# Experts stage: the low parts of the down weights computed by VectorE instead of GpSimd, and VectorE's step in another order

## The reference

```python
h = modulate(rmsnorm(x, norm_ffn), sh2, sc2)
s = sigmoid(h @ w_router)                      # 64 scores; 4 of 8 groups, then 6 experts for each token
gates = sel / sum(sel) * 2.5
routed[token] += gate * (silu(h @ w1[e]) * (h @ w3[e])) @ w2[e]      # for each of the 6 experts
shared = (silu(h @ ws1) * (h @ ws3)) @ ws2
x = x + g2 * (routed + shared);  out = rmsnorm(x, norm_final)
```

## Time and profile before

| | |
|---|---|
| three runs, us | 2855.18 (median), 2844.31, 2860.29 |
| profiled execution, us | 2856.53 |
| its span, us | 2854.9 |
| mean granted clock of TensorE | 0.955 of 2.4 GHz |
| busy, us (share of span) | TensorE 2541.4 (89%), VectorE 1692.9 (59%), GpSimd 1364.5 (48%), ScalarE 1014.7 (36%) |
| HBM | 224 GB/s over the span |

### The profile page before, as it was taken

How to read it: one execution, slowest core, us unless ns; L and a number is a source line. 1 busy time by engine, 2 the same in 40 slices (tenths; PEclk the granted TensorE clock), 3 DMA queues, 4 the chain that set the end, 5 groups by cost and what they waited for, 6 DMA issues and landing times. The chain is left out here.

```text
span 2854.9 us, 52119 instructions
## 1 busy us (share of the span) xinstructions
PE 2541.4 (89%) x11953; PEld 2029.2 (71%) x11954; DVE 1692.9 (59%) x2579; ACT 1014.7 (36%) x1615; POOL 1364.5 (48%) x1136
## 2 busy tenths in 40 slices
PE   7999999999849899589999999999998999989991
PEld 4787777777638777478777777777776788767780
DVE  4664554574236777554855575675588644686643
ACT  3212433323212222212543353443356422453422
POOL 1210025612245666421655665665577644576644
PEclk9999999999969999699999999999999999999995
DMA  7775768574456554445986887987799866698747
GB/s 274 305 259 203 265 214 309 196 276 166 163 209 232 170 202 159 149 111 139 340 258 162 248 274 191 271 268 190 200 282 351 285 168 155 183 317 259 209 105 270
DMA packets 247800, 641.42 MB, mean 225 GB/s; under 512 B 32876, under 2 KB 46512, under 8 KB 232240
## 3 DMA queue, kind: packets, MB, share of 16 engines
q1 hardware_dynamic: 188736, 459.72, 44.8%
q0 software_dynamic: 58992, 180.78, 25.9%
HBM read 463.08 MB, written 177.33 MB: 224 GB/s over the span
## 5 line engine op out<-in xcount | busy, mean ns | idle before, releaser
L2154 DVE TENSOR_TENSOR w_exp_lo<-w_exp,w_exp_hi (+1 forms) x256 | 401.8, 1604 | 74.5 <-ACT w_exp_hi L2093 65.5
L2093 ACT ACTIVATE w_exp_hi<-w_exp (+1 forms) x256 | 260.9, 1056 | 220.4 <-issue 130.5
L2280 PE MATMUL ps_h<-w_exp_hi,x_exp_t_hi 128*128 (+1 forms) x1216 | 312.6, 399 | 26.1 <-ACT w_exp_hi L2093 20.3
L2010 POOL TENSOR_TENSOR w_exp_lo<-w_exp,w_exp_hi (+1 forms) x130 | 321.9, 2500 | 13.2 <-ACT w_exp_hi L2097 10.1
L2280 PE MATMUL ps_h<-w_exp_lo,x_exp_t_hi 128*128 (+1 forms) x1216 | 311.6, 398 | 16.9 <-DVE w_exp_lo L2154 16.9
L2280 PE MATMUL ps_h<-w_exp_hi,x_exp_t_lo 128*128 (+1 forms) x1216 | 321.6, 407 | 0.0
L2280 PEld LDWEIGHTS ps_h<-w_exp_hi,x_exp_t_hi 128*128 128x128 f32 x1216 | 228.1, 189 | 88.9 <-ACT w_exp_hi L2093 20.5
L2070 POOL DMA_INDIRECT sum_d<-w_shared_raw,give x136 | 246.1, 1810 | 91.1 <-DVE w_shared_raw L2192 42.9
L2280 PEld LDWEIGHTS ps_h<-w_exp_lo,x_exp_t_hi 128*128 128x128 f32 x1216 | 228.4, 189 | 77.2 <-issue 22.6
L1134 PE MATMUL ps_p<-wa_hi,hx_split 128*128 128x512 f32 x1088 | 279.1, 403 | 4.1 <-DVE kvqg_out L100 3.2
L2060 POOL DMA_DIRECT2D give<-list_d x136 | 76.7, 564 | 399.2 <-issue 391.6
(11 more groups left out here) (270 smaller groups left out, 4390.6 us busy)
## 6 DMA issues: line engine op xcount, KB each, us to landing
w_exp<-in_experts SPq DMA_DIRECT2D x386, 512.0 KB, 7.6
hx_split<-hx_d SPq DMA_DIRECT2D x54, 1024.0 KB, 5.7
rec_m<-rec_d SPq DMA_DIRECT2D x16, 1536.0 KB, 8.8
hx_d<-hx_split SPq DMA_DIRECT2D x18, 1024.0 KB, 5.5
wm_rest<-in_w_mod_rest POOLq DMA_DIRECT2D x16, 1024.0 KB, 5.9
rec_d<-kvqg_out SPq DMA_DIRECT2D x48, 256.0 KB, 4.4
xt<-in_xt POOLq DMA_DIRECT2D x18, 512.0 KB, 8.8
rec_d<-kt_kvf_out SPq DMA_DIRECT2D x32, 256.0 KB, 5.4
```

The source lines that it names most:

```text
L2010: pool.tensor_tensor(w[1][:, piece(e, i)].bitcast(F32R), raw(e, i), w[0][:, piece(e, i)], ALU.subtract).then_inc(wd_lo, 1)
L2093: act.activation(w[0][:, piece(e, i)].bitcast(F32R), raw(e, i), ACT.Copy).then_inc(gu_hi, 1)
L2154: dve.tensor_tensor(w[1][:, piece(e, i)].bitcast(F32R), raw(e, i), w[0][:, piece(e, i)], ALU.subtract).then_inc(gu_lo, 1)
L2280: last = pe.matmul(out, x[:, j * P:(j + 1) * P].bitcast(F32R), w_part[:, bass.ds(w_at + j * stride, 512)].bitcast(F32R), start=(start and ...
```

## The change

The splits of the down weights (`split`) leave GpSimd's program and come to VectorE's as `split_d`. VectorE's order in step k becomes: pieces 0 and 1; weighing of tile k - 2; low part of h of tile k - 1; piece 2; gating; low part of x; piece 3; then, where tile k - 1 was the first of its expert, the two down pieces. VectorE therefore looks up the change at k - 1 too. The last two tiles are weighed behind the loop.

```diff
@@ gpsimd
-            def split(e, i):
-                pool.wait_ge(wd_hi, e * N_D + i - N_GU + 1)
-                pool.tensor_tensor(w[1][:, piece(e, i)].bitcast(F32R), raw(e, i), w[0][:, piece(e, i)],
-                                   ALU.subtract).then_inc(wd_lo, 1)
-
-            for i in range(N_GU, N_GU + N_D):
-                split(0, i)
...
-            for i in range(N_GU, N_GU + N_D):
-                split(1, i)
...
             def step(k, par, r):
-                before = change(pool, k - 1) if not isinstance(k, int) or k > NT else None
                 gather(k + 2, par, r + 1)
                 load_take(k + 3, 1 - par, r + 1 + par)
-                if before is not None:
-                    at_change(pool, before, split, range(N_GU, N_GU + N_D))
@@ vector
+            def split_d(e, i):
+                dve.wait_ge(wd_hi, e * N_D + i - N_GU + 1)
+                dve.tensor_tensor(w[1][:, piece(e, i)].bitcast(F32R), raw(e, i), w[0][:, piece(e, i)],
+                                  ALU.subtract).then_inc(wd_lo, 1)
...
                 here = change(dve, k)
-                at_change(dve, here, split, range(3))
+                before = change(dve, k - 1) if not isinstance(k, int) or k > 0 else None
+                at_change(dve, here, split, range(2))
+                if not isinstance(k, int) or k > 1:
+                    weigh(k - 2, par, None if isinstance(k, int) else r - 1)
                 if not isinstance(k, int) or k > 0:
                     copy_ht(k - 1, 1 - par)
+                at_change(dve, here, split, range(2, 3))
...
                 at_change(dve, here, split, range(3, N_GU))
                 if not isinstance(k, int) or k > 0:
-                    weigh(k - 1, 1 - par, None if r is None or (isinstance(k, int) and k == NT) else r - (1 - par))
+                    wait(dve, d_done, k - 1)
+                    at_change(dve, before, split_d, range(N_GU, N_GU + N_D))
...
             for i in range(N_GU):
                 split(0, i)
+            for i in range(N_GU, N_GU + N_D):
+                split_d(0, i)
             n = iterations(dve, step, after)
+            weigh(n * 2 + (NT - 2), 0, n - 1)
             copy_ht(n * 2 + (NT - 1), 1)
             weigh(n * 2 + (NT - 1), 1, n - 1)
```

## The result

The changed kernel took 2907.14 us (median of 4 runs, 2900.46 to 2911.72) against 2857.73 us for the kernel before on the same chip (4 runs). The ratio is 1.0181, 95% interval 1.0142 to 1.0219: slower. I had forecast 2836 us and a range up to 2880; the time that came lies 5 us from the one that rival B gave, 2912.

What follows compares the result with a forecast made beforehand. TensorE, busy 89%, was taken to lose 145 us at expert changes in the routed part. Waits of -11 us times 1.6 gave -18; with -3.4 (start) and +2 (loads) some -19, so 2836 us, range 2804 to 2880.

Steps and rivals of the forecast that it cites:

- rival B: Step after each change step outside long runs: gather behind the late weighing, 68 us of waits, 2912 us; chance 0.22.
- The lock of VectorE and GpSimd: VectorE's weight subtractions: GpSimd's subtractions stop them; 97 us of waiting in VectorE's busy time go, maximum below 1.3 us.
- VectorE's added work and the start: VectorE takes 130 more subtractions, busier by about 62 us net; the wait at 1222.70, ahead of the routed part, shrinks: -3.4 us.
- Low part of the weights: TensorE's 16.9 us of waits for VectorE's low part of the weights: -8 us, ends 0 and -16.9.
- Saturated runs: Long runs of expert changes: VectorE ends the down subtractions later than GpSimd did, +9 us of waits, ends -5 and +36.
- Register loads: VectorE's lookup of the step before, two loads more a step: mostly hidden, 2 us, bounds 0 and 69.
- Low part of h: TensorE's waits for VectorE's low part of h: -12 us in all, ends 0 and -39.2.
- Gather: TensorE's 33.8 us gather wait: -20 from GpSimd's freed time, +20 (ends 0 and +80) from the weighing behind two subtractions.
- The price of a wait, 1.6: Routed part: one us of TensorE wait costs 145/90 = 1.6 us of time.

Runs made afterwards that it cites:

- e2: The kernel before with only VectorE's new order; the down subtractions stay on GpSimd, two lookups a step: 1.0301 of the kernel before.
- e7: The changed kernel with the weighing of tile k - 2 ahead of pieces 0 and 1, still behind the four lookups: 0.9954 of the kernel before.
- e13: The changed kernel with the weighing first in VectorE's step, ahead of the lookups and of pieces 0 and 1: 0.9864 of the kernel before.
- e4: The kernel before with two more lookups a step on VectorE, result unused, nothing else: 1.0048 of the kernel before.
- e3: The changed kernel with 3 + 1 lookups in a round of two steps instead of 4 + 4: 1.0048 of the kernel before.
- e1: The kernel before with the down subtractions moved to VectorE, its old order kept (weighing last, behind them), four lookups a step: 0.9953 of the kernel before.
- e11: e16's kernel with a memset of 2.4 us on GpSimd ahead of each gather: 0.9875 of the kernel before.
- e14: e16's kernel with a memset (1.83 us median) on GpSimd ahead of each scatter, behind its wait for the weighing: 1.0257 of the kernel before.
- e15: As e14 with the memset ahead of each scatter half as long, 0.98 us: 1.0027 of the kernel before.
- e16: e1 with 3 + 1 lookups in a round instead of 4 + 4, no memset: 0.9886 of the kernel before.
- e8: The changed kernel with GpSimd issuing the gather one tile further ahead, before the scatter instead of behind it: 1.0663 of the kernel before.

## Why the prediction was wrong

*The lock of VectorE and GpSimd: right.* All 256 gate and up subtractions now take 1211 to 1228 ns; in e2, where GpSimd keeps its own, the longest takes 6077. The rule of the Trainium skill ("SBUF — State Buffer", Who interferes with whom) that the prediction used agrees with both.

*VectorE's added work and the start: right in the main.* GpSimd's busy time is down by 318 us (320 forecast). VectorE's is up by 37 (62 forecast); its weight subtractions alone take 58 more by the view's lines (306.9 + 153.1 for 401.8), and the rest I did not trace. The wait of TensorE at its first down products fell from 7.78 to 2.87 us, but its wait for ScalarE's high part of x before that grew from 2.01 to 4.53; together the shared expert's steps are 2.5 us shorter, for my 3.4.

*Low part of the weights: better.* I took -8 of the 16.9 us; all of it went.

*Saturated runs: smaller.* I took +9 us of waits, some 14 us of time; the run of 11 is 130.3 us for 130.6, and all eight long runs together are 2.8 us longer.

*Register loads: failed, the second cause.* I counted two added loads per step and took 2 us, since the pieces that followed the lookups had no idle time ahead. I did not ask what the reorder makes of the loads that were there. The first piece starts at a median of +3.0 to +4.3 in the change steps of the kernel before, the changed one, e7 and e13, whatever stands ahead; the weighing can start at +0.2, and the change put it behind the loads in every step, quiet ones too. In the rows of the changed kernel that is 4.58 us without work; moved ahead of them (e7 to e13) the weighing gives 0.9% back, some 25 us. The loads that were added cost their own share besides (e4: 0.5%, 14 us, inside my bounds of 0 and 69).

*Low part of h: failed.* I took -12; it came out +3. e3 and e7 show what held it up: with fewer lookups it is 11.2 us, with the weighing ahead of the pieces 23.7. The gain was there, and the lookups and the weighing ahead of it ate it; I had charged 0.2 to 0.3 us for the second and nothing for the first.

*Gather: the step that failed.* The term was -20 for GpSimd's freed time and +20 for the late weighing, together 0; it measured +53.8. Of the first part e1 shows 6 us in the old order (33.8 to 27.7), and the changed kernel against e2 13 to 18 in the new one. The second, from e1 to the changed kernel, is +55 to +60 for my +20; its mechanism is rival B as written: I gave it 42 steps with 68 us of waits, and 43 steps have 55.1. The gather went out at a median of +10.8 in change steps (I had +9.7). I put its landing "near the short end" because fewer loads are released ahead of it; 38 gathers instead of 60 do take 8 us or more, as I had reckoned, but that did not help. The landing that matters hangs on the scatter ahead (e11, e14), and the scatter hangs on the weighing and on the landing of the scatter before. That loop takes 11.6 us beside a burst (scatters at 1485.99 and 1497.54 in the changed kernel, each some 1.0 us behind its list, which waits for the landing of the scatter before) and about 8.2 in quiet ones (an estimate: the 10.01 of e14's rows less the memset's 1.83). It recovers its delay in quiet steps only as far as the weighing lets it: where the scatter waits for the weighing there, it goes out at a median of +2.5 before and +5.6 after. The 182.1 us that the scatter now waits for the weighing (80 times) were 42.9 (27 times) before. In change steps the scatter goes out at +8.4 (median) for +5.3 before. That the lost reserve is what carries this over is argued from these medians; e14 and e15 show only that a later scatter costs this kind of wait.

*The price of a wait, 1.6: held.* 136 quiet steps are 1292 us, so 200 us are lost for 134 us of waits, 1.5.

So the mechanism of B was on the page with its place and its price and had a chance of 0.22. What argued it down, a short landing counted from the gather's own issue, was counted from the wrong start. That B's time is met within 5 us is partly luck. Its waits add up to +37 us and +40 came, but from other terms: the gather +54 for +48, the low part of h +3 for -12, the weights -17 for -8, the saturated runs next to nothing for +9. The loads ahead of the weighing are not in it.

## What to carry to other kernels

When an instruction is moved, ask what it now stands behind on its engine's sequencer, register loads included, and price that for every step, not for the busy ones alone. A result that feeds a chain of serialized DMAs (here the accumulating scatter) belongs first in its engine's step, ahead of lookups and of work that waits for others anyway: two moved lines turned 1.8% slower into 1.4% faster. Where a DMA is issued close behind another one in the same queue (here 2.0 to 3.7 us), ask whether its landing counts from the other's issue.

## What the runs showed of the hardware

A register load from SBUF on VectorE's sequencer takes 0.31 us as a median but up to 1.6, the long ones almost only where the weighing does not stand ahead of the loads (143 of 537 over 0.6 us in the changed kernel, 3 of 537 in e13). From the start of the first of two loads to the end of the second it is 1.0 us (median in the kernel before): one more pair a step costs it 0.5% (e4). An indirect gather issued 2.0 or 3.7 us behind an indirect scatter of the same queue is usable 11.7 us after the scatter in either case (means over the gathers that TensorE waits for, e16 and e11), and 6.4 us after its own issue where no scatter is just ahead (e8). An indirect scatter with its landing and the next one's list and issue is a chain of some 8 us in quiet steps; a pause of 0.98 us in it costs 1.4%, of 1.83 us 3.7%, and one of 2.4 us ahead of the gather beside it nothing (e15, e14, e11). That the descriptors wait in the queue is the reading that fits; it was not seen directly.
